# Half of the attention branch's merge moved beside the recurrence and cross attention, in a hybrid decoder layer on eight cores

## The reference, cut to what matters

```
h = rms_norm(x);  proj = h @ w_in          # split into m_*, a_*, c_*, gates
# A: mLSTM, 4 heads of 256: conv + silu on q,k; chunkwise matrix recurrence; norm; gates  -> hm
# B: latent attention, 8 heads: q,k = 128 plain + 64 rotary columns, v = 128
q_rope = [x1*cos - x2*sin, x2*cos + x1*sin]           # x1, x2: the halves of the 64
p = softmax(q k^T / sqrt(192), causal);  ha = (p @ v) * silu(a_z)
# C: cross attention of 4 heads into 256 memory tokens  -> hc
merged = sigmoid(g_m)*(hm @ w_br_m) + sigmoid(g_a)*(ha @ w_br_a) + sigmoid(g_c)*(hc @ w_br_c)
out = rms_norm(x + merged @ w_out, final_norm)
```

## Time and profile before

| | |
|---|---|
| median of 3 runs | 2845.86 us |
| the three runs | 2841.17, 2845.86, 3097.22 us |
| the profiled execution | 2839.96 us, span of its slowest core 2838.9 us |
| spans of the eight cores | 2823.2 to 2838.9 us |
| granted TensorE clock | 0.990 to 0.992 of full speed on each core |
| PE busy | 2734.3 us, 96% of the span |
| DVE, ACT, POOL busy | 1083.0, 812.4, 498.6 us |

### The profile page before, as it was taken

How to read it: one execution, slowest core, us unless ns; L and a number is a source line. 1 busy time by engine, 2 the same in 40 slices (tenths; PEclk the granted TensorE clock), 3 DMA queues, 4 the chain that set the end, 5 groups by cost and what they waited for, 6 DMA issues and landing times.

```text
span 2838.9 us, 42235 instructions; the slowest of 8 cores (2823.2 to 2838.9 us)
## 1 busy us (share of the span) xinstructions
PE 2734.3 (96%) x14325; PEld 1364.3 (48%) x14325; DVE 1083.0 (38%) x2039; ACT 812.4 (29%) x1676; POOL 498.6 (18%) x605
## 2 busy tenths in 40 slices
PE   6989999999999999989889899999999999999998
PEld 3544444674547644445444444444444444444443
DVE  4634466448475466356553321111111111110433
ACT  5532244335353344245553311111111111110211
POOL 0002200000100111234331022222222222221000
PEclk9999999999999999999999999999999999999999
DMA  7537534533335323446344645545474654457552
GB/s 227 142 93 173 174 86 114 112 81 104 101 74 140 96 64 72 84 125 162 121 119 123 182 82 78 78 76 78 77 162 77 108 78 75 78 76 121 201 200 82
DMA packets 145733, 319.03 MB, mean 112 GB/s; under 512 B 14961, under 2 KB 73265, under 8 KB 138353
## 3 DMA queue, kind: packets, MB, share of 16 engines
q0 software_dynamic: 42192, 134.79, 29.4%
q1 hardware_dynamic: 100450, 171.04, 18.7%
q10 hardware_dynamic: 2880, 10.49, 1.1%
HBM read 378.56 MB, written 72.48 MB: 159 GB/s over the span
## 4 chain that ended last, share of the span: by engine, by line
PE 88%; DMA 5%; DVE 2%; ACT 2%; issue 2%; SPq 0%; DVEq 0%; POOL 0%; ACTq 0%; POOLq 0%
PE bk L290 87%; DMA xo<-x 1%; DMA cq<-CQT 1%; DMA w<-wA 1%; PE bk L489 1%; DVE e L310 0%; DMA mv<-MV 0%; DMA QRT<-ob 0%; DMA QNT<-ob 0%; ACT junk L294 0%; ACT e L294 0%; ACT hmt L294 0%; DVE y L310 0%; PE bk L514 0%; DMA xt<-x 0%
## 5 line engine op out<-in xcount | busy, mean ns | idle before, releaser
L290 PE MATMUL bk<-hT,wg 128*128 128x512 bf16 x3072 | 681.3, 379 | 0.0
L290 PE MATMUL bk<-w,hT 128*128 128x512 bf16 (+1 forms) x3072 | 602.5, 346 | 18.2 <-DMA w<-wA 6.2
L290 PE MATMUL bk<-hT,w 128*128 128x512 bf16 x2112 | 493.2, 382 | 4.3 <-ACT hr L298 2.2
L290 PEld LDWEIGHTS bk<-hT,wg 128*128 128x128 bf16 x3072 | 300.6, 98 | 361.0 <-issue 1.4
L290 PEld LDWEIGHTS bk<-w,hT 128*128 128x128 bf16 x3072 | 298.4, 98 | 261.0 <-issue 28.8
L294 ACT ACTIVATE sh<-bk 128x512 f32<-128x512 f32 x184 | 109.8, 597 | 850.7 <-PE bk L290 850.7
L290 PE MATMUL bk<-hb,wb 128*128 128x512 bf16 x1536 | 346.7, 379 | 0.0
L290 PEld LDWEIGHTS bk<-hT,w 128*128 128x128 bf16 x2112 | 206.7, 99 | 232.2 <-issue 11.1
L310 DVE SCALAR_TENSOR_TENSOR tm<-sh,bk 128x512 f32<-128x512 f32 x124 | 85.3, 688 | 559.9 <-PE bk L290 558.5
L290 PEld LDWEIGHTS bk<-hb,wb 128*128 128x128 bf16 x1536 | 150.2, 98 | 181.0
L294 ACT ACTIVATE Pa<-bk 128x512 bf16<-128x512 f32 (+1 forms) x320 | 167.1, 533 | 214.7 <-PE bk L290 213.2
(11 more groups left out here) (179 smaller groups left out, 2352.6 us busy)
## 6 DMA issues: line engine op xcount, KB each, us to landing
wg<-wGB POOLq DMA_DIRECT2D x96, 512.0 KB, 5.5
w<-wA POOLq DMA_DIRECT2D x48, 516.0 KB, 11.0
wb<-wGB POOLq DMA_DIRECT2D x96, 256.0 KB, 3.9
xt<-x SPq DMA_DIRECT2D x16, 1024.0 KB, 16.2
xo<-x SPq DMA_DIRECT2D x16, 1024.0 KB, 30.9
out<-xo SPq DMA_DIRECT2D x16, 1024.0 KB, 10.2
rba<-RDA SPq DMA_DIRECT2D x32, 256.0 KB, 3.3
wo<-wOUT POOLq DMA_DIRECT2D x4, 2048.0 KB, 18.0
```

What stands on the lines that cost most here:

```text
L290: fw.op("pe", lambda e: e.matmul(bk[o] if not isinstance(o, bass.AP) else o, lhsT=lhsT, rhs=rhs, start=start, stop=stop), reads=reads, wri ...
```

## The change

Four things are changed.

1. **Rotary.** The rotary columns are laid out as both heads' x1 and then both heads' x2 (on the host), and the swapped copy is dropped, so `uq` has 384 columns in place of 512 for each pair. The new `rotate` reads one PSUM bank three times on DVE: all rows times cos, and the upper and the lower half crossed over times sin. The shared key is treated alike, stored with 128 rows, and loaded into the two zero-padded tiles `krs` in two pieces each.
2. **Softmax sums.** `finish` splits `den` into a bf16 part hi (DVE copy) and the rest lo (POOL subtract), multiplies both with a 128x128 matrix of twos (2 matmuls), and takes the reciprocal as exp(-ln(x)) with two ACT instructions. The store to DRAM and the broadcast load are gone. The ticks are 1, 4, 5, 7 in place of 1, 4, 8, 13.
3. **Recurrence.** The ring of six banks is split in three: one bank, three and two. P2n comes after the last state update of the chunk. One buffer less for the decay rows.
4. **Merge.** A new `d1_gen` between `mid_gen` and `d_gen` computes the 16 units of the attention branch for the first half of the tokens and stores the products in DRAM (AP). `d_gen` does the other 80 units and loads those products into `acc`. The list DU gives the order of all 96 units, and weight loads run along it across the border; `wb` has three buffers. The ratios of the recurrence and cross attention are 0.24 and 0.5.

```diff
@@ -677,6 +677,14 @@
             def part(o, c, bk, r_bk, first):
                 evac_copy(o[:, c], bk[:, 0:512], [r_bk], [o.r] if first else [], [] if first else [o.r])
 
+            def rotate(o, tb, bk, r_bk):
+                cols = slice(tb * 512, (tb + 1) * 512)
+                t1, t2 = t1s.next(), t1s.next()
+                tt("dve", t1[:], bk[:, 0:512], cosT[:, cols], ALU.mult, [r_bk, cosT.rs[tb]], [t1.r])
+                tt("dve", t2[0:64, :], bk[64:128, 0:512], sinT[64:128, cols], ALU.mult, [r_bk, sinT.rs[tb]], [t2.r])
+                tt("dve", t2[64:128, :], bk[0:64, 0:512], sinT[0:64, cols], ALU.mult, [r_bk, sinT.rs[tb]], [], [t2.r])
+                tt("pool", o[:, cols], t1[:], t2[:], ALU.add, [t1.r, t2.r], [o.r] if tb == 0 else [], [o.r] if tb else [])
...
                 o = ob.next()
                 for tb in range(4):
                     cols = slice(tb * 512, (tb + 1) * 512)
-                    t1, t2 = t1s.next(), t1s.next()
                     yield from fm_unit(wb, 256, 128, lambda kc: cqnT[:, kc, cols], [cqnT.rs[tb]],
-                                       lambda bk, r_bk: tt("dve", t1[:], bk[:, 0:512], cosT[:, cols], ALU.mult, [r_bk, cosT.rs[tb]], [t1.r]), q=4)
-                    yield from fm_unit(wb, 384, 128, lambda kc: cqnT[:, kc, cols], [cqnT.rs[tb]],
-                                       lambda bk, r_bk: tt("dve", t2[:], bk[:, 0:512], sinT[:, cols], ALU.mult, [r_bk, sinT.rs[tb]], [t2.r]), q=4)
-                    tt("pool", o[:, cols], t1[:], t2[:], ALU.add, [t1.r, t2.r], [o.r] if tb == 0 else [], [o.r] if tb else [])
+                                       lambda bk, r_bk: rotate(o, tb, bk, r_bk), q=4)
                 fw.dma("sp", QRT_d[pr * 128:(pr + 1) * 128, :], o[:], reads=[o.r], accs=[dr("QRT", pr)])
...
             vxs = tiles("vx", 1, [128, 16, 128], BF16, top=True)
             for i in range(2):
-                lo = slice(64, 128) if i == 0 else slice(0, 64)
-                hi = slice(0, 64) if i == 0 else slice(64, 128)
-                fw.op("dve", lambda e: e.memset(krs[i][lo, :], 0.0), writes=[krs[i].r])
-                fw.dma("sp", krs[i][hi, :], KRT_d, reads=[dr("KRT")], accs=[krs[i].r])
+                fw.op("dve", lambda e: e.memset(krs[i][:], 0.0), writes=[krs[i].r])
+                for lo in (32 * i, 64 + 32 * i):
+                    fw.dma("sp", krs[i][lo:lo + 32, :], KRT_d[lo:lo + 32, :], reads=[dr("KRT"), krs[i].r] if lo == 32 * i else [dr("KRT")], accs=[krs[i].r])
...
             def finish(h, qb, acc, po, r_po):
...
-                rd, rt_, u, rb = rds.next(), rts.next(), us.next(), rbs.next()
+                hi, lo, u, rb = his.next(), los.next(), us.next(), rbs.next()
...
                 def f1():
-                    for b in range(4):
-                        mm(dn, r_dn, (slice(None), slice(b, b + 1)), acc[:, b * 128:(b + 1) * 128], twof[:], True, True, [acc.r, RM])
-                    fw.op("dve", lambda e: e.reciprocal(out=rd[:], in_=dn[:, 0:4]), reads=[r_dn], writes=[rd.r])
+                    copy("dve", hi[:], acc[:], [acc.r], [hi.r])
+                    tt("pool", lo[:], acc[:], hi[:], ALU.subtract, [acc.r, hi.r], [lo.r])
                     tt("dve", u[:], po[:, 0:512], az[:, cols], ALU.mult, [r_po, az.r], [u.r])
 
                 def f2():
-                    fw.op("pe", lambda e: e.transpose(out=dn[0:4, 128:256], in_=rd[:], identity=identf[:]), reads=[rd.r, RC], writes=[r_dn])
-                    copy("dve", rt_[:], dn[0:4, 128:256], [r_dn], [rt_.r])
-                    fw.dma("sp", RDA_d[h:h + 1, cols].rearrange("o (b p) -> (o b) p", p=128), rt_[:], reads=[rt_.r], accs=[dr("RDA", h, qb)])
+                    mm(dn, r_dn, (slice(None), slice(None)), twob[:], hi[:], True, False, [hi.r, RM])
+                    mm(dn, r_dn, (slice(None), slice(None)), twob[:], lo[:], False, True, [lo.r, RM])
 
                 def f3():
-                    fw.dma("sp", rb[:], RDA_d[h:h + 1, cols].partition_broadcast(128), reads=[dr("RDA", h, qb)], writes=[rb.r])
+                    act(rb[:], dn[:], AF.Ln, [r_dn], [rb.r])
+                    act(rb[:], rb[:], AF.Exp, [rb.r], [rb.r], scale=-1.0)
...
                 later(1, f1)
                 later(4, f2)
-                later(8, f3)
-                later(13, f4)
+                later(5, f3)
...
-            misc = bub = bob = Ring(SB)
+            misc, bub, bob = Ring(SB[5:6]), Ring(SB[2:5]), Ring(SB[0:2])
...
-            B2s = tiles("mb", 3, [128, 4, 128], F32, top=True)
+            B2s = tiles("mb", 2, [128, 4, 128], F32, top=True)
...
-                    fw.dma("sp", B2s[c % 3][:].rearrange("p a b -> p (a b)"), BH_d[c:c + 1].rearrange("o a b -> o (a b)").partition_broadcast(128), reads=[dr("BH")], writes=[B2s[c % 3].r])
+                    fw.dma("sp", B2s[c % 2][:].rearrange("p a b -> p (a b)"), BH_d[c:c + 1].rearrange("o a b -> o (a b)").partition_broadcast(128), reads=[dr("BH")], writes=[B2s[c % 2].r])
...
-                loads_b(c + 3)
+                loads_b(c + 2)
...
                         yield 0.67
-                        P2n(c)
+                P2n(c)
                 if c + 2 < 16:
...
+        DU = [(0, c, 1) for c in range(16)] + [(0, c, b) for c in range(16) for b in (0, 2)] + [(1, c, b) for c in range(16) for b in range(3)]
+        dld = {"g": 3, "b": 0}
...
+        def gate_unit(u, ring, gates):
+            th, c, b = DU[u]
...
+            gates[u] = []
+            for tb in range(2):
+                bk, r_bk = DB.next()
+                for kc in range(16):
+                    mm(bk, r_bk, (slice(None), slice(None)), w[:, kc, :], hcol(kc, 2 * th + tb), kc == 0, kc == 15, [w.r] + rhg(2 * th + tb))
+                    if kc % 8 == 7:
+                        yield 8 * MM
+                sg = ring.next()
+                act(sg[:], bk[:], AF.Tanh, [r_bk], [sg.r], scale=0.5)
+                gates[u].append(sg)
+            gload()
...
+        def d1_gen():
+            mem.release(wst["last"], *P["e16"].items, *P["e32"].items)
+            h1 = P["hb1"] = mem.alloc("hb1", [128, 8, 1024], BF16)
+            wb = P["wb"] = tiles("wb", 3, [128, 8, 128], BF16)
+            sgs, ps = Ring(tiles("sa", 4, [128, 512], F32)), Ring(tiles("pa", 2, [128, 512], F32))
+            for j in range(4):
+                c = slice(j * 2048, (j + 1) * 2048)
+                fw.dma("sp", h1[:].rearrange("p a b -> p (a b)")[:, c], HAT_d[0].rearrange("p a b -> p (a b)")[:, c], reads=[dr("HAT", 0)], writes=[h1.r] if j == 0 else [], accs=[h1.r] if j else [])
+            for _ in range(3):
+                bload()
+            gates = {}
+            yield from gate_unit(0, sgs, gates)
+            for c in range(16):
+                if c + 1 < 16:
+                    yield from gate_unit(c + 1, sgs, gates)
+                w2, sg2 = wb[c % 3], gates.pop(c)
+                for tb in range(2):
+                    bk, r_bk = DB.next()
+                    for kc in range(8):
+                        mm(bk, r_bk, (slice(None), slice(None)), w2[:, kc, :], h1[:, kc, tb * 512:(tb + 1) * 512], kc == 0, kc == 7, [w2.r, h1.r])
+                    t = ps.next()
+                    stt(t[:], sg2[tb][:], 1.0, bk[:], ALU.add, ALU.mult, [sg2[tb].r, r_bk], [t.r])
+                    fw.dma("sp", AP_d[c, tb], t[:], reads=[t.r], accs=[dr("AP", c, tb)])
+                    yield 8 * MM
+                bload()
+            mem.release(*sgs.items, *ps.items)
...
         def d_gen():
-            mem.release(wst["last"], *P["e16"].items, *P["e32"].items)
             LA = 4
-            units = [(th, c, b) for th in range(2) for c in range(16) for b in range(3)]
-            wg = P["wg"]
-            sgs = tiles("sg", 2 * LA, [128, 512], F32)
-            ld = {"g": 3, "b": 0}
+            U0, units = 16, DU[16:]
+            wg, wb = P["wg"], P["wb"]
+            sgs = tiles("sg", 2 * LA, [128, 512], F32, top=True)
+            ld = {"a": 0}
             gates = {}
 
...
+            def aload():
+                c = ld["a"]
+                if c < 16:
+                    ld["a"] += 1
+                    for tb in range(2):
+                        fw.dma("sp", acc[2 * (c % 2) + tb][:], AP_d[c, tb], reads=[dr("AP", c, tb)], writes=[acc[2 * (c % 2) + tb].r])
...
             sring = Ring(sgs)
-            wb = [mem.alloc("wb%d" % i, [128, 8, 128], BF16) for i in range(4)]
-            for _ in range(4):
-                bload()
             yield ("need", "HM1")
-            hb = [mem.alloc("hb0", [128, 4, 8, 256], BF16), mem.alloc("hb1", [128, 8, 1024], BF16), P["hb2"]]
+            hb = [mem.alloc("hb0", [128, 4, 8, 256], BF16), P["hb1"], P["hb2"]]
             hload(0, 0)
-            hload(0, 1)
+            hload(1, 1)
             for u in range(LA):
-                for i, v in enumerate(gate_unit(u, sring)):
...
             yield ("need", "HC1")
             DB.items = banks[:]
             tmps = Ring(tiles("tm", 2, [128, 512], F32))
```

(47 more changed lines are left out.)

75 lines of the change are left out of this document (22 added, 53 removed).

## The result

The changed kernel takes 2851.52 us against 2844.96 us before (medians of 18 runs each, taken together). In some executions the cores of one or both dies ran at a lower granted clock throughout; ratios, intervals and stage times leave such executions and such cores out. The ratio is 1.0027, its 95% interval 1.0014 to 1.004. That is 0.3% slower, inside the 2% band, and 51.5 us above the forecast of 2800 us, outside its range of 2780 to 2818. The profiled execution took 2849.96 us.

The account below looks back on a forecast made before the run. PE, with work in 96% of the span, was taken as the bound; 2840.0 less 4 (rotary), 17 (softmax sums) and 22 (recurrence and cross attention) gave 2797 us, plus 3 towards the median 2800 us, range 2780 to 2818.

Parts of the forecast that it names:

- recurrence and cross attention: Those two stages: moved dense work, split rings and P2n's new place cut waits and low clock, 22 us won.
- Split rings: Recurrence: separate PSUM rings, one of three causes together taking 19 us of waits away, with 5 put back.
- P2n behind the updates: Recurrence: P2n after the state updates, one of three causes together taking 19 us of waits away.
- More dense work between: Recurrence: 10 dense steps a chunk for 7, one of three causes together taking 19 us of waits away.
- Smaller dense banks, +3: Recurrence and cross attention: smaller waits of the dense banks, 3 us won.
- d1, -4: Recurrence and cross attention: d1_gen's two banks and 8-matmul parts halve the time before a bank's reuse, 4 us lost.
- The second rival, given back: Whole kernel: uq bound by stores, ACT takes back the softmax gain, recurrence waits renamed; 11 us won, 2832 us, chance 0.13.
- Cross attention: Cross attention: waits for cq fall below 9 us despite shared queues, 4 us won.
- Rotary: The uq stage: 64 matmuls fewer, DVE keeps pace, stores give part back; 4 us won, bounds 0 and 13.9.
- Softmax sums: Beside causal attention: 15.7 us of matmuls and 9 of waits won, 8 lost to ACT table loads; 17 us won.
- the third rival: Softmax sums: ACT's table-load bursts make PE late by 2 us, 5.4 us each with low clock; 2962 us, chance 0.07.
- Everything comes through: Whole kernel: stores do not hold uq, ACT bursts fit gaps, moved work closes most waits; 71 us, 2772 us, chance 0.32.

Follow-up runs that it names:

- i2: The changed kernel with only the recurrence's order at a chunk's end made tail, P1e, P2n; 2814.25 us, ratio 0.9892 to the kernel before.
- e2: The changed kernel with the recurrence's banks in one ring of six again; recurrence 429.4 us, ratio 0.9963 to the kernel before.
- i1: h1 with the recurrence's banks in one ring of six; 2772.21 us, ratio 0.9746 to the kernel before.
- g4: e4 with P2n moved behind the last state update, one ring, no d1; recurrence, cross attention and rest 1435.7 us against 1437.6, one run.
- e3: The changed kernel with P2n back before the last two state updates, split rings kept; recurrence 460.6 us, ratio 1.009 to the kernel before.
- g3: The changed kernel with one ring and the old ratios 0.34 and 0.7; 2829.2 us in one run.
- h1: g2 with P1e put ahead of P2n in the recurrence; 2787.35 us, ratio 0.9802 to the kernel before.
- h2: h1 without d1, the merge and the ratios as before the change; ratio 0.9896 to the kernel before.
- g2: g1 with six ob tiles and the cq loads a step earlier; uq 42.6 us on three cores, recurrence 438.1, cross attention 112.7.
- e4: The kernel before with only the softmax sums changed; ratio 0.9961 to the kernel before.
- g1: The changed kernel with krs loads not waiting for each other, uq's plain copies on ACT, tail ahead of P2n and P1e; 2835.8 us, one run.

## Why the prediction failed, point by point

**The step that failed** is the one on recurrence and cross attention: "with split rings, P2n behind the updates and more dense work between [...] I take 19 us away". I had read the waits for `Cf`, `hmt` and `hm` as PE wanting a bank of a shared ring, a queueing of several parts, and priced P2n behind the updates as part of the cure. But there it stands right ahead of P1e, and that order is what cost the time: in 14 of the 16 chunks one chain runs through two in-order queues, fourteen small operations on DVE, `DT` behind them, four exponentials on ACT, and the copies and tanh queued behind those. ACT's waits for `DT` rise from 5.6 us to 45.9, and turning the order round takes 29.9 us off the recurrence (i2). I had priced that P2n gets out of the way of the updates, and put at nothing what it then stands in the way of.

The other parts of that sentence fare differently. *Split rings*: a loss of 11.7 us (e2), of 15.2 once the order is right (i1). *P2n behind the updates*, with one ring and the old merge: 2 us (g4); with split rings its old place is worse still (e3, +19.5), since there it delays `Cf` itself. *More dense work between*: nothing in the order of the change (g3), but 26 us together with the moved branch once the order is right (h1 against h2). That part is not shown wrong; the order hid it. *Smaller dense banks, +3, and d1, -4*: not seen apart. What made the waits for `Cf`, `hmt` and `hm` in the kernel *before* stays open: the chain through `DT` was not there, and P2n stood ahead of `Cf` instead.

From the change to g2 PE's waits in the recurrence stay at 36 to 46 us, core by core, while their names go from `hm` (19.5) to `Cf` (20.3). I should have tested them for that: a chain that sets the pace looks like many small waits for different things.

The second rival, given back, had the recurrence keep its waits under other names; that was right, but its price of 8 us is a gain, and I allowed a loss of at most 15 there. The loss was 21.3. Not all of it is explained: e4, whose recurrence is that of before, already has a sum 9.7 us above before's, and g4 one 7.8 above. What moved there when attention became shorter was not tried.

**Cross attention.** Forecast: waits for `cq` under 9 us, +4 from shared queues. Measured: 12.5 us in 4 waits, with a clock of 0.94. That the load is held by a store waiting for DVE on SP's queue I named, and excused as "needed a chunk or a step later"; with a load that leaves 14 us after the one before it (1611.21, 1625.57) and PE at the next step already at 1627.7, a step is not enough. One step earlier takes the waits for `cq` away and gives 13.6 us over g1.

**Rotary.** Forecast: the stage 7 us shorter, 4 of them in the sum; it became 2.2 shorter. The group of PE in this stage, changed kernel:

```profile
L290 PE MATMUL bk<-cqnT,w 128*128 128x512 bf16 x192 | 44.4, 387 | 13.3 <-ACT ob L298 7.8 <-DVE ro L303 5.4
```

And DVE's three products there:

```profile
289.56 0.68 DVE L303 TENSOR_TENSOR ro<-bk,cosT 128x512 f32<-128x512 f32 x1
290.27 1.41 DVE L303 TENSOR_TENSOR ro<-bk,sinT 64x512 f32<-64x512 f32 x2
291.71 0.69 DVE L303 TENSOR_TENSOR ro<-bk,cosT 128x512 f32<-128x512 f32 x1
```

A 64-row product costs what a 128-row one does, as taken. But they start 0.72 us apart (289.56 to 291.71 is three), where I took the 0.60 of the earlier trace rows. A pair is 12 x 0.72 + 4 x 0.60 = 11.0 us of DVE, over PE's 10.4 and not 9.6 under it: DVE is the bound I had ruled out, hence `ro` 5.4, which falls to under 1 us once ACT makes the copies (g1). The rest is the store queue, which I had marked as the danger, with the krs loads in it but not their wait for one another, 16.56 us. Copies on ACT and six tiles bring the stage to 42.6 us on three cores of g2; in h1 and i1 it lies between 42.6 and 50.3 us, and the slow cores read there still wait 3 to 5 us for copies into `ob`.

**Softmax sums.** This step held. On the core of the earlier trace rows attention took 855.9 us, and it takes 838.9 now, 17.0 less, as forecast, and nearly by its terms. An estimate from that core's busy time, waits and clock: 16.4 us of matmul work (forecast 15.7), 9.1 for the two waits with their low clock (9), and 8.5 of new waits and low clock (8). The full 17 is that core's, though. On four cores the stage was 852.5 us before, so it is 13.5 less there, and 14.4 in the median. Those cores have the same two waits for `rta`, but no low clock behind the first, which cost core 2 3.4 us. Core 0 of the kernel before, beside the earlier trace rows:

```profile
463.60 1.02 PE L290 MATMUL bk<-twof,den 128*128 128x1 f32 x8 [1.99 <-DVE rta L300]
464.48 1.89 PE L290 MATMUL bk<-hT,w 128*128 128x512 bf16 x8
```

The f32 matmuls and the transpose are gone. The new work on ACT, as groups, 335 to 1163 us:

```profile
L294 ACT ACT_TABLE_LOAD x52 | 66.7, 1283 | 10.9 <-PE bk L290 10.2
...
L294 ACT ACTIVATE rba<-rba 128x512 f32<-128x512 f32 x32 | 20.2, 630 | 2.9
L294 ACT ACTIVATE rba<-bk 128x512 f32<-128x512 f32 x32 | 19.1, 596 | 0.3
```

52 loads were in the forecast's 50 to 64. They made PE late by at most the 6.2 us of its 7 waits for `Pa` (longest 3.3); forecast 8. One burst on ACT's timeline, changed kernel:

```profile
360.40 1.28 ACT L294 ACT_TABLE_LOAD   x1
361.70 0.60 ACT L294 ACTIVATE rba<-bk 128x512 f32<-128x512 f32 x1
362.38 0.63 ACT L294 ACTIVATE rba<-rba 128x512 f32<-128x512 f32 x1
363.03 1.28 ACT L294 ACT_TABLE_LOAD   x1
```

The logarithm starts 1.30 us after the load does, and the burst is 3.9 us, as priced (3.8). The Trainium skill ("ScalarE: Activation LUTs", section "What ACT_TABLE_LOAD costs") gives 1283 ns for the load, as here, and about 1380 ns more for a drain, which this trace does not show; the measurement decides, and the third rival with it.

**The ranking.** *Everything comes through* at 2772 us is what i1 reaches, with other edits and by another division (uq 11.8 us shorter, attention 13.9, the other three 42.5). That so much waiting could go was read rightly; that the edit as written would free it was not, and that the two numbers agree is luck.

## What to carry to other kernels

Where several short waits with different releasers add up to tens of microseconds, follow one of them back through each in-order queue before pricing any: ask what stands ahead of the releaser in its own queue, and whether that is urgent. Put the head of the next chain ahead of long runs of small dependent operations, and when you move such a run out of one chain's way, look at what it now stands in front of. And never let an in-order DMA queue hold a load that is due behind a store or a second load whose wait is long.

## What the runs showed of the hardware that was not expected

- The same DVE product of 128x512 f32 with PSUM starts 0.60 us after its predecessor in one sequence (301.55 to 302.15) and 0.72 us in another (289.56 and the two of 64 rows behind it). Half the rows save nothing. Why the spacing differs was not tried.
- Small dependent DVE operations of 0.16 us start 0.27 us apart: 14 of them hold the queue for 3.6 us.
- A DVE reciprocal of 128x512 f32 takes 3.35 us, five times a product of that size (0.68).
- A wait of PE can cost more than its length: after 5.22 us four matmuls take 1.86 us in place of 1.03, and the stretches of the change with such waits show a granted clock of 0.94, so part of them at 1.2 GHz; the same stretches of i1, with few waits, show 1.00. But the price is not fixed: after the same wait of 1.99 us in the kernel before, eight matmuls take 3.57 us on core 2 and the usual 1.89 on core 0.
